# Gate and up: three of eight pairs of row tiles by seven products instead of two, with ScalarE copying the product banks out and GpSimd adding them

## The chip, the cores and the metric

The kernel runs on one core of a Trainium2 chip. The metric is the device time of one execution in microseconds (us). TensorE multiplies into PSUM (8 banks of 128x512 fp32), ScalarE (ACT) and VectorE (DVE) read PSUM and SBUF, GpSimd (POOL) works on SBUF, and SyncE (SP) issues the weight loads. Each engine has its own instruction stream, in order, and they meet at semaphores.

## The reference

The program is two layers of a four-mixer attention block and then one block with attention, convolution and a feed-forward part, on 256 tokens of width 2048. Only the feed-forward part matters here:

```python
h = rms_norm(x, norm2_g)                     # 256 x 2048
x = x + (silu(h @ w_gate) * (h @ w_up)) @ w_down   # w_gate, w_up: 2048 x 5632
```

All of it is fp32. A product of fp32 accuracy is made of three matmuls on rounded halves: high x high, high x low, low x high.

## The kernel before

**Tiling.** Gate and up are computed in 11 steps of 512 columns (`FFN_STEPS`). In a step the 2048 rows of a weight are 16 row tiles of 128, taken as 8 pairs. A load (`raw`, a ring of 4 buffers of 512 KB) brings one pair of one weight. ScalarE rounds it (`split_high`: `wh`), VectorE subtracts (`split_low`: `wl`), and TensorE multiplies. `wh` and `wl` are rings of 4 slots: the high part of unit n waits until unit n-4 is multiplied, the low part waits for the high part, the multiply waits for the low part. I call the two splits of unit n hi(n) and lo(n).

**An eight.** A pair of one weight is a unit of 12 matmuls of 512 columns. Both weights together need 24.

**A seven.** Steps 1 to 9 (`seven_step`) compute some pairs otherwise. The 2x2 blocks (two halves of the tokens by two row tiles) times (two row tiles by gate and up) are multiplied with seven products instead of eight (Winograd's form of Strassen): 21 matmuls for both weights. It takes four units, here called parts p0 to p3 (6, 3, 6 and 6 matmuls). p0 and p1 split raw weights. p2 and p3 split sums of weights that VectorE forms in `sum_weights` after lo(p1), from both raw buffers of the pair, which are free only then (`weights_summed`). Four products are accumulated in banks 4 to 7, called mixes; the rest goes straight to the accumulators of gate (banks 0, 1) and up (banks 2, 3).

**A step before.** 20 units: g0 g1 u0 u1, transposes, g2 u2, seven S0 (units 6 to 9), g3 u3, seven S1 (12 to 15), g4 g5 u4 u5. The eight transposes (`turn_act`) bring the product of the previous step into banks 4 and 5; ScalarE and VectorE read them out as `ah` (`act_turned`) and `al` (`act_low`). TensorE waits for both before it writes the mixes:

```python
if n == FIRST_SEVEN:                       # unit 6
    pe.wait_ge(act_mid_done, pl.slots + 2)
    pe.wait_ge(dve_mid_done, pl.slots + 2)
```

After S1 ScalarE copies one mix bank (`first_mix`), VectorE adds the others (`add_mixes`), adds the accumulators (`gate_sum`, `up_of_mixes`), ScalarE applies silu, and VectorE forms the product.

**Loads.** SyncE issues the loads of a step in the order of `plan.raws`. Load k waits for the one 4 places earlier to be done with: an eight's by its low part, a seven's two by its weight sums. The order is one queue, so a load that waits holds every later one.

## Time and profile before

| what | value |
|---|---|
| median of three runs | 1956.89 us (1956.38 to 1957.09) |
| the profiled execution | 1956.36 us, span of the core 1954.6 us |
| TensorE busy | 1939.9 us (99% of the span) |
| VectorE, ScalarE, GpSimd busy | 1365.2, 1000.6, 80.0 us |
| granted TensorE clock | 1.0 of full speed |
| the nine steps with sevens | from about 1284 us to 1673 us of the span |

Busy time of TensorE counts overlapping matmuls as one stretch. A row of the timeline is start, duration, engine, line, operation, out<-in, count, and in brackets the idle time ahead of it on that engine with the instruction that ended it.

### The profile page before, as it was taken

How to read it: one execution, taken by the hardware profiler on the slowest of the kernel's cores; microseconds unless marked ns; L12 is line 12 of the kernel's file. 1: busy time of each engine (PE TensorE's matmuls, PEld its weight loads, DVE VectorE, ACT ScalarE, POOL GpSimd, SP SyncE). 2: the span in 40 equal slices, each digit the busy share in tenths (PEclk: the TensorE clock that was granted, in tenths of full speed). 3: DMA queues.
4: the chain of work that ended last, by engine and by line, in shares of the span. 5: the costliest groups of instructions: out<-in, count | busy, mean ns of one | idle time of the engine just before them, and what ended most of it. 6: DMA issues, size and time to landing. Idle time of an engine off the chain costs nothing.

```text
span 1954.6 us, 26389 instructions
## 1 busy us (share of the span) xinstructions
PE 1939.9 (99%) x9568; PEld 1621.3 (83%) x9568; DVE 1365.2 (70%) x1619; ACT 1000.6 (51%) x1328; POOL 80.0 (4%) x125
## 2 busy tenths in 40 slices
PE   9999999999999999999999999999999999999998
PEld 7888888887888888888787878888888888888887
DVE  6595655556667664655657986768888888678777
ACT  6365444444555453444555555645555555445453
...
PEclk9999999999999999999999999999999999999999
...
GB/s 288 199 228 130 155 169 167 185 202 162 256 183 187 148 132 176 183 195 192 144 194 156 151 145 168 184 179 196 202 194 188 193 192 194 205 183 194 226 199 157
DMA packets 204538, 360.75 MB, mean 185 GB/s; under 512 B 13201, under 2 KB 53184, under 8 KB 204176
## 3 DMA queue, kind: packets, MB, share of 16 engines
...
q8 instruction: 65, 1.06, 0.2%
...
## 4 chain that ended last, share of the span: by engine, by line
PE 97%; ACT 1%; DVE 1%; DMA 0%; issue 0%; ACTq 0%; SPq 0%; DVEq 0%
PE psum L758 23%; PE psum L760 23%; PE psum L759 23%; PE psum L765 6%; PE psum L767 3%; PE psum L1305 2%; PE psum L1307 2%; PE psum L1306 2%; PE psum L1551 1%; PE psum L874 1%; PE psum L1239 1%; PE psum L888 1%; PE psum L863 1%; PE psum L1020 1%; PE psum L1808 0%; PE psum L782 0%
## 5 line engine op out<-in xcount | busy, mean ns | idle before, releaser
L723 DVE TENSOR_TENSOR wl<-raw,wh 128x1024 fp32r<-128x1024 f32 (+2 forms) x595 | 694.7, 1192 | 341.4 <-ACT wh L715 327.9
L715 ACT ACTIVATE wh<-raw 128x1024 fp32r<-128x1024 f32 (+2 forms) x595 | 603.1, 1032 | 536.0 <-PE psum L760 386.9
L758 PE MATMUL psum<-wh,xs 128*128 128x512 f32 (+2 forms) x1440 | 559.4, 389 | 4.5 <-DVE xs L1058 4.2
L760 PE MATMUL psum<-wh,xs 128*128 128x512 f32 (+2 forms) x1440 | 552.9, 384 | 0.0
L759 PE MATMUL psum<-wl,xs 128*128 128x512 f32 (+2 forms) x1440 | 552.5, 384 | 0.0
L758 PEld LDWEIGHTS psum<-wh,xs 128*128 128x128 f32 x1440 | 270.6, 188 | 60.8 <-DVE xs L1058 7.1
L760 PEld LDWEIGHTS psum<-wh,xs 128*128 128x128 f32 x1440 | 270.5, 188 | 53.0
L759 PEld LDWEIGHTS psum<-wl,xs 128*128 128x128 f32 x1440 | 270.8, 188 | 51.2
L765 PE MATMUL psum<-xs,wh 128*128 128x512 f32 x512 | 181.4, 398 | 0.0
L767 PE MATMUL psum<-xs,wl 128*128 128x256 f32 x512 | 143.3, 280 | 0.0
L758 PE MATMUL psum<-wh,mh 128*128 128x512 f32 x360 | 141.6, 393 | 0.0
L760 PE MATMUL psum<-wh,ml 128*128 128x512 f32 x360 | 140.2, 389 | 0.0
L759 PE MATMUL psum<-wl,mh 128*128 128x512 f32 x360 | 140.1, 389 | 0.0
L765 PEld LDWEIGHTS psum<-xs,wh 128*128 128x128 f32 x512 | 96.1, 188 | 22.4
L767 PEld LDWEIGHTS psum<-xs,wl 128*128 128x128 f32 x512 | 96.7, 189 | 0.1
L758 PE MATMUL psum<-wh,ah 128*128 128x512 f32 x248 | 96.6, 389 | 0.0
L760 PE MATMUL psum<-wh,al 128*128 128x512 f32 x248 | 96.5, 389 | 0.0
L759 PE MATMUL psum<-wl,ah 128*128 128x512 f32 x248 | 96.5, 389 | 0.0
L1332 DVE TENSOR_TENSOR wl<-raw,wh 128x1024 fp32r<-128x1024 f32 (+1 forms) x60 | 56.2, 956 | 37.4 <-ACT wh L1325 37.4
L1325 ACT ACTIVATE wh<-raw 128x1024 fp32r<-128x1024 f32 (+1 forms) x60 | 50.8, 847 | 59.0 <-PE psum L760 44.0
L758 PEld LDWEIGHTS psum<-wh,mh 128*128 128x128 f32 x360 | 67.6, 188 | 14.3 <-issue 0.6
L760 PEld LDWEIGHTS psum<-wh,ml 128*128 128x128 f32 x360 | 67.6, 188 | 14.3
...
## 6 DMA issues: line engine op xcount, KB each, us to landing
...
```

What stands on the lines that cost most here:

```text
L715: act.activation(shaped(wh[:, n % SPLIT_SLOTS], unit)[:, 0:k, 0:unit.n], shaped(buffer, unit)[:, 0:k, 0:unit.n], ACT.Copy).then_inc(hi_don ...
L723: dve.tensor_tensor(out=shaped(wl[:, n % SPLIT_SLOTS], unit)[:, 0:k, 0:unit.n], in0=shaped(buffer, unit)[:, 0:k, 0:unit.n], in1=shaped(wh[ ...
L758: pe.matmul(o, ah_[:, kt, tok], hi_w, start=first, stop=False)
L759: pe.matmul(o, ah_[:, kt, tok], lo_w, start=False, stop=False)
L760: ins = pe.matmul(o, al_[:, kt, tok], hi_w, start=False, stop=last)
L765: pe.matmul(o.rearrange("p (i t) -> p i t", i=2), hi_w[:, f], xs[:, :, kt, :], start=first, stop=False, skip_group_check=True)
L767: ins = pe.matmul(o[:, 0:T], lo_w[:, f], xh[:, kt, :], start=False, stop=last, skip_group_check=True)
L1305: pe.matmul(o, x_hi, hi_w, start=first, stop=False)
L1306: pe.matmul(o, x_hi, lo_w, start=False, stop=False)
L1307: ins = pe.matmul(o, x_lo, hi_w, start=False, stop=last)
L1325: act.activation(wh[:, n % SPLIT_SLOTS, 0:source.shape[1], :], source, ACT.Copy).then_inc(hi_done, 1)
L1332: dve.tensor_tensor(out=wl[:, n % SPLIT_SLOTS, 0:k, :], in0=source, in1=wh[:, n % SPLIT_SLOTS, 0:k, :].bitcast(F32), op=ALU.subtract).then ...
```

## The change

Three of the eight pairs become sevens (pairs 1, 3, 5), in nine steps. Units of a step are now 24: 0 g0, 1 u0, transposes, 2 g1, 3 to 6 S0, 7 u1, 8 g2, 9 to 12 S1, 13 u2, 14 g3, 15 to 18 S2, 19 u3, 20 and 21 the halves of g4, 22 and 23 the halves of u4. The names g1, u1 and so on count the eights alone. The u of a pair is loaded ahead of the seven and used after it (`+u1` in the order). The transposes go to banks 6 and 7, and TensorE waits for `ah` and `al` at p2 of S0 (unit 5), the first part that writes these banks. ScalarE copies all four mix banks to SBUF, GpSimd makes the four additions of 512 columns and the last product of 1024 columns, and ScalarE multiplies the silu by the token's scale.

```diff
-GATE_UP_SEVENS = (3, 6)
-GATE_UP_ORDER = ("g0", "g1", "u0", "u1", "g2", "u2", "S0", "g3", "u3", "S1", "g4", "g5", "u4", "u5")
+GATE_UP_SEVENS = (1, 3, 5)
+GATE_UP_ORDER = ("g0", "u0", "g1", "+u1", "S0", "u1", "g2", "+u2", "S1", "u2", "g3", "+u3", "S2", "u3", "G4", "U4")
...
-FIRST_SEVEN, SEVENS_END, GATE_END = 6, 16, 18
+FIRST_SEVEN, SEVENS_END, GATE_END, TURN_UNITS = 3, 19, 22, 2
...
+            def pool_mix(i):
...
+                pool.wait_ge(s("act_mixes"), 3 * (i - FIRST_SEVEN_STEP) + 1)
+                stand_alone(pool, "pool")
+                add(1, 0, 1)
+                pool.drain()
+                pool.wait_ge(s("act_mixes"), 3 * (i - FIRST_SEVEN_STEP) + 2)
+                stand_alone(pool, "pool")
+                add(2, 2, 1)
+                pool.drain().then_inc(s("pool_mixes"), 1)
+                add(1, 3, 1)
+                add(3, 3, 2)
+                pool.drain().then_inc(s("pool_mixes"), 1)
+                pool.wait_ge(s("act_mixes"), 3 * (i - FIRST_SEVEN_STEP) + 3)
+                pool.wait_ge(dve_mid_done, ffn_place(i + 1).slots + 1)
+                stand_alone(pool, "pool")
+                pool.tensor_tensor(out=act_a[:, :, :], in0=x_mixes[:, 1:4:2, :], in1=silu[:, :, :], op=ALU.mult)
+                pool.drain().then_inc(s("pool_mixes"), 1)
...
             def seven_step(i):
                 pl = ffn_place(i)
                 for n, unit in enumerate(GATE_UP.units):
-                    if n == 2:
+                    if n == 1:
                         pe.wait_ge(dve_mid_done, pl.slots + 1)
                     if n == FIRST_SEVEN:
+                        pe.wait_ge(s("sums_low"), 1)
+                    if n == FIRST_SEVEN + 2:
                         pe.wait_ge(act_mid_done, pl.slots + 2)
                         pe.wait_ge(dve_mid_done, pl.slots + 2)
-                        pe.wait_ge(s("sums_low"), 1)
...
-                    if n == SLOT_UNITS - 1:
+                    if n == TURN_UNITS - 1:
+                        if not isinstance(i, int):
+                            pe.wait_ge(s("pool_mixes"), 3 * (i - FIRST_SEVEN_STEP))
                         pe_stage(pl, 0, turn_act)
...
-            def first_mix(pl):
+            def copy_mixes(pl):
 
                 act.wait_ge(unit_used, SPLIT_SLOTS + pl.units + SEVENS_END)
-                act.activation(x_mixes[:, 0, :], psum[:, 4, :], ACT.Copy).then_inc(s("first_mix"), 1)
+                act.activation(x_mixes[:, 0:2, :], psum[:, 4:6, :], ACT.Copy).then_inc(s("act_mixes"), 1)
+                act.activation(x_mixes[:, 2:4, :], psum[:, 6:8, :], ACT.Copy).then_inc(s("act_mixes"), 1)
...
-                    ins = act.activation(silu[:, tb, :], x_mixes[:, 2 * tb, :], ACT.Silu, scale=x_rstd[:, tb:tb + 1])
-                ins.then_inc(s("gate_ready"), 1)
+                    ins = act.activation(silu[:, tb, :], silu[:, tb, :], ACT.Silu, scale=x_rstd[:, tb:tb + 1])
+                act.drain()
+                for tb in range(TB):
+                    ins = act.activation(silu[:, tb, :], silu[:, tb, :], ACT.Copy, scale=x_rstd[:, tb:tb + 1])
+                ins.then_inc(s("act_mixes"), 1)
...
             def seven_step(i):
                 pl = ffn_place(i)
+                dve_mid(pl, -1, 0, up_part if isinstance(i, int) else lambda: up_of_mixes(i - 1))
                 for n, unit in list(enumerate(GATE_UP.units))[AHEAD:]:
                     if unit.part is None:
                         split_low(pl, n, unit)
                     else:
                         seven_low(pl, n, unit)
-                    if n == 2:
-                        dve_mid(pl, -1, 0, up_part if isinstance(i, int) else lambda: up_of_mixes(i - FIRST_SEVEN_STEP))
-                    elif n == 7:
-                        dve_mid(pl, 0, SLOT_UNITS, lambda: act_low(i))
-                    elif n == GATE_END - 1:
-                        add_mixes(i, pl)
+                    if n == 6:
+                        dve_mid(pl, 0, TURN_UNITS, lambda: act_low(i))
```

On VectorE, in the loop over the steps, from the low part of S0's p1 on. Before (`wl` is a low part, `x_weight_sums` the weight sums, `al` the read-out of the transposes):

```order
L1332 TENSOR_TENSOR wl<-raw,wh 128x512 [waits hi_done]
L1344 TENSOR_TENSOR x_weight_sums<-raw 128x1024
L1347 TENSOR_TENSOR x_weight_sums<-raw,x_weight_sums 128x512
L1349 TENSOR_TENSOR x_weight_sums<-raw,x_weight_sums 128x512
L836 REGISTER_ALU [waits unit_used]
L2400 ISA [waits stage_done,ffn_high]
L2400 TENSOR_TENSOR al<-psum,ah 128x1024
L1329 REGISTER_ALU
L1332 TENSOR_TENSOR wl<-x_weight_sums,wh 128x1024 [waits hi_done]
L1329 REGISTER_ALU
L1332 TENSOR_TENSOR wl<-x_weight_sums,wh 128x1024 [waits hi_done]
```

In the changed kernel:

```order
L1372 TENSOR_TENSOR x_weight_sums<-raw,x_weight_sums 128x512
L1352 REGISTER_ALU
L1355 TENSOR_TENSOR wl<-x_weight_sums,wh 128x1024 [waits hi_done]
L1352 REGISTER_ALU
L1355 TENSOR_TENSOR wl<-x_weight_sums,wh 128x1024 [waits hi_done]
L857 REGISTER_ALU [waits unit_used]
L2465 ISA [waits stage_done,ffn_high]
L2465 TENSOR_TENSOR al<-psum,ah 128x1024
L741 REGISTER_ALU
L744 TENSOR_TENSOR wl<-raw,wh 128x1024 [waits hi_done]
L741 REGISTER_ALU
L744 TENSOR_TENSOR wl<-raw,wh 128x1024 [waits hi_done]
```

`al` stood between the weight sums and the low parts of p2 and p3; now it stands behind both, and u1's low part (the first `wl<-raw` behind it) follows.

On TensorE, in the loop, at the first seven. Before, from the last matmul ahead of S0 on (`x_sum_high` is a sum of x blocks):

```order
L760 MATMUL psum<-wh,xs 128x512
L1952 REGISTER_ALU
L1301 REGISTER_ALU [waits sums_low,dve_mid_done,act_mid_done]
L1305 MATMUL psum<-wh,xs 128x512 [waits lo_done]
L1306 MATMUL psum<-wl,xs 128x512
L1307 MATMUL psum<-wh,xs 128x512
L1305 MATMUL psum<-wh,xs 128x512
L1306 MATMUL psum<-wl,xs 128x512
L1307 MATMUL psum<-wh,xs 128x512
L1301 REGISTER_ALU
L1305 MATMUL psum<-wh,x_sum_high 128x512 [waits lo_done]
```

In the changed kernel, from the last matmuls of S0's p0 on:

```order
L1328 MATMUL psum<-wh,xs 128x512
L1329 MATMUL psum<-wl,xs 128x512
L1330 MATMUL psum<-wh,xs 128x512
L1324 REGISTER_ALU
L1328 MATMUL psum<-wh,x_sum_high 128x512 [waits lo_done]
L1329 MATMUL psum<-wl,x_sum_high 128x512
L1330 MATMUL psum<-wh,x_sum_low 128x512
L2011 REGISTER_ALU
L1324 REGISTER_ALU [waits dve_mid_done,act_mid_done]
L1328 MATMUL psum<-wh,x_sum_high 128x512 [waits lo_done]
L1329 MATMUL psum<-wl,x_sum_high 128x512
```

The wait for `dve_mid_done`, which `al` raises, stood ahead of p0 and is now ahead of p2 (the second `x_sum_high` row with a wait).

On SyncE, in the loop, the loads ahead of and at S1. Before, from the load of g3 (load 8) on:

```order
L1399 REGISTER_ALU
L1402 DMA raw<-in_w_up_dram 128x2x512 [waits lo_done]
L1401 ISA
L1402 ISA [waits weights_summed]
L1402 DMA raw<-in_w_gate_dram 128x2x512
L1402 DMA raw<-in_w_up_dram 128x2x512 [waits weights_summed]
L1399 REGISTER_ALU
L1402 ISA [waits lo_done]
L1402 DMA raw<-in_w_gate_dram 128x2x512
L1399 REGISTER_ALU
L1402 ISA [waits lo_done]
L1402 DMA raw<-in_w_gate_dram 128x2x512
```

In the changed kernel, from the load of g2 (load 6) on:

```order
L1428 REGISTER_ALU
L1431 ISA [waits lo_done]
L1431 DMA raw<-in_w_gate_dram 128x2x512
L1428 REGISTER_ALU
L1431 DMA raw<-in_w_up_dram 128x2x512 [waits lo_done]
L1430 REGISTER_ALU
L1431 ISA [waits weights_summed]
L1431 DMA raw<-in_w_gate_dram 128x2x512
L1431 DMA raw<-in_w_up_dram 128x2x512 [waits weights_summed]
L1428 REGISTER_ALU
L1431 ISA [waits lo_done]
L1431 DMA raw<-in_w_gate_dram 128x2x512
```

Ahead of S1's two loads, which wait for S0's weight sums, now stands load 7 (u2), whose `lo_done` is that of unit 7 (u1), multiplied after S0. Before, the loads ahead of them (g3, u3) waited for units 4 and 5, which come before S0. Load 11 (u3) stands in the same way ahead of S2's two loads and waits for unit 13.

## Rows read from the trace of the kernel before

**Rows 1.** The page: span, busy time, granted clock, the chain that ended last.

```profile
span 1954.6 us, 26389 instructions
PE 1939.9 (99%) x9568; PEld 1621.3 (83%) x9568; DVE 1365.2 (70%) x1619; ACT 1000.6 (51%) x1328; POOL 80.0 (4%) x125
...
PEclk9999999999999999999999999999999999999999
...
PE 97%; ACT 1%; DVE 1%; DMA 0%; issue 0%; ACTq 0%; SPq 0%; DVEq 0%
```

**Rows 2.** Windows, one middle step: us, busy by engine, clock, DMA share, GB/s.

```profile
1402.90:1446.10 43.20, 43.20 (x195) 35.66 (x194) 35.53 (x35) 22.75 (x25) 0.00 (x0) 1.00 0.61 194
```

**Rows 3.** Timeline of TensorE, the same step: first matmul behind S1, first transpose.

```profile
1402.66 0.39 PE L758 MATMUL psum<-wh,xs 128*128 128x512 f32 x1
...
1424.43 0.27 PE L1239 MATMUL psum<-ident,act 128*128 128x128 f32 x1
```

**Rows 4.** Timeline of ScalarE, the same step.

```profile
1402.87 0.60 ACT L2334 ACTIVATE x_mixes<-psum 128x512 f32<-128x512 f32 x1 [1.39 <-PE psum L1307]
...
1411.12 1.34 ACT L2340 ACTIVATE silu<-x_mixes,small 128x512 f32<-128x512 f32 x2 [1.45 <-DVEq L839]
...
1421.90 1.06 ACT L1325 ACTIVATE wh<-raw 128x1024 fp32r<-128x1024 f32 x1 [1.66 <-PE psum L760]
1424.63 0.63 ACT L1325 ACTIVATE wh<-raw 128x512 fp32r<-128x512 f32 x1 [1.66 <-PE psum L760]
1425.67 1.03 ACT L2301 ACTIVATE ah<-psum 128x1024 f32 x1 [0.41 <-PE psum L1239]
...
1446.09 0.60 ACT L2334 ACTIVATE x_mixes<-psum 128x512 f32<-128x512 f32 x1 [1.39 <-PE psum L1307]
```

**Rows 5.** Timeline of VectorE, the same step.

```profile
1413.44 1.23 DVE L723 TENSOR_TENSOR wl<-raw,wh 128x1024 fp32r<-128x1024 f32 x1 [0.97 <-ACT wh L715]
1414.59 1.22 DVE L2400 TENSOR_TENSOR x_mixes<-psum,x_mixes 128x1024 f32<-128x1024 f32 x1
...
1423.00 1.23 DVE L1332 TENSOR_TENSOR wl<-raw,wh 128x1024 fp32r<-128x1024 f32 x1 [1.49 <-ACT wh L1325]
1425.29 0.69 DVE L1332 TENSOR_TENSOR wl<-raw,wh 128x512 fp32r<-128x512 f32 x1 [1.07 <-ACT wh L1325]
...
1428.20 0.69 DVE L1349 TENSOR_TENSOR x_weight_sums<-raw,x_weight_sums 128x512 f32<-128x512 f32 x1
1429.35 1.23 DVE L2400 TENSOR_TENSOR al<-psum,ah 128x1024 f32 x1 [0.46 <-issue]
1430.76 2.52 DVE L1332 TENSOR_TENSOR wl<-x_weight_sums,wh 128x1024 fp32r<-128x1024 f32 x2 [0.18 <-issue]
...
1439.90 0.69 DVE L1349 TENSOR_TENSOR x_weight_sums<-raw,x_weight_sums 128x512 f32<-128x512 f32 x1
1440.79 1.23 DVE L1332 TENSOR_TENSOR wl<-x_weight_sums,wh 128x1024 fp32r<-128x1024 f32 x1 [0.20 <-issue]
```

**Rows 6.** Timeline of TensorE's weight loads, at the first matmul of S0.

```profile
1430.79 0.19 PEld L1305 LDWEIGHTS psum<-wh,xs 128*128 128x128 f32 x1 [0.29 <-issue]
```

**Rows 7.** SyncE's queue, the loads of S1's pair; then each one's time to landing.

```profile
1429.09 0.37 SPq L1402 DMA_DIRECT2D raw<-in_w_gate_dram  x1
1429.56 0.41 SPq L1402 DMA_DIRECT2D raw<-in_w_up_dram  x1
...
DMA to landing us min/median/max: 3.8/3.8/3.8
...
DMA to landing us min/median/max: 4.6/4.6/4.6
```

**Rows 8.** Timelines of GpSimd and VectorE, where the two overlap and where they don't.

```profile
494.66 1.22 DVE L723 TENSOR_TENSOR wl<-raw,wh 128x1024 fp32r<-128x1024 f32 x1 [2.23 <-ACT wh L715]
...
494.86 1.08 POOL L974 TENSOR_SCALAR small<-small 128x1 f32<-128x1 f32 x1
...
497.46 0.19 POOL L974 TENSOR_SCALAR small<-small 128x1 f32<-128x1 f32 x1 [0.78 <-ACTq L1014]
...
1057.35 0.21 POOL L974 TENSOR_SCALAR small<-small 128x16 f32<-128x16 f32 x1 [75.17 <-DVEq L2751]
```

More of the change, by code:

```diff
@@ L115, in __init__ @@
         self.by_rows = False
-        self.raw = self.part = None
+        self.raw = self.part = self.half = None
 def slots_of(units):
@@ L238, in eight, with eight_in_halves @@
         unit = Unit(self.weights[g], ((0, GN),), kts, "t", g, self.operand, self.ktiles, first, last)
-        unit.raw = self.load(g, kts, len(self.units))
+        if (g, kts) not in self.raws:
+            self.load(g, kts, None)
+        unit.raw = self.raws.index((g, kts))
+        self.released[unit.raw] = len(self.units)
         self.units.append(unit)
+    def eight_in_halves(self, g, kts, last):
+        raw = self.load(g, kts, len(self.units) + 1)
+        for half, kt in enumerate(kts):
+            unit = Unit(self.weights[g], ((0, GN),), (kt,), "t", g, self.operand, self.ktiles, False, last and half == 1)
+            unit.raw, unit.half = raw, half
+            self.units.append(unit)
     def seven(self, j):
@@ L287, in __init__ @@
                 self.seven(int(kind[1]))
+            elif kind[0] in "GU":
+                pair = eights[int(kind[1])]
+                self.eight_in_halves("GU".index(kind[0]), (2 * pair, 2 * pair + 1), pair == eights[-1])
+            elif kind[0] == "+":
+                pair = eights[int(kind[2])]
+                self.load("gu".index(kind[1]), (2 * pair, 2 * pair + 1), None)
             else:
@@ L713, in split_high @@
             act.wait_ge(unit_used, place.units + n + 1)
-            k = len(unit.kts)
+            k, k0 = len(unit.kts), unit.half or 0
             act.activation(shaped(wh[:, n % SPLIT_SLOTS], unit)[:, 0:k, 0:unit.n],
-                           shaped(buffer, unit)[:, 0:k, 0:unit.n], ACT.Copy).then_inc(hi_done, 1)
+                           shaped(buffer, unit)[:, k0:k0 + k, 0:unit.n], ACT.Copy).then_inc(hi_done, 1)
         def split_low(place, n, unit):
@@ L1292, in of_sum @@
             def of_sum(which):
+                if unit.operand == "x" and unit.pair == 2:
+                    return x_sum_high_2[:, which, :], x_sum_low_2[:, which, :]
                 return sum_h[:, unit.pair, which, :], sum_l[:, unit.pair, which, :]
@@ L1397, in load_plan @@
                     before = k - RAW_SLOTS if k < RAW_SLOTS else plan.released[k - RAW_SLOTS]
-                    if isinstance(before, int):
+                    if plan is GATE_UP and k < 2 and not isinstance(i, int):
+                        sp.wait_ge(s("weights_summed"), (i - FIRST_SEVEN_STEP) * (2 * len(GATE_UP_SEVENS)))
+                    elif plan is GATE_UP and k < RAW_SLOTS and not isinstance(i, int):
+                        sp.wait_ge(lo_done, RAW_SLOTS + place.units + plan.released[k - RAW_SLOTS] - len(plan.units) + 1)
+                    elif isinstance(before, int):
                         sp.wait_ge(lo_done, RAW_SLOTS + place.units + before + 1)
@@ L1930, in turn_act @@
             def turn_act():
-                return pe_turn_mix(act_a, 0)
+                return pe_turn_mix(act_a, 2)
             def ffn_step(i, first):
@@ L1944, in ffn_step @@
                         h = FFN_SLOT_ENDS.index(n + 1)
+                        if h == 0 and not first:
+                            pe.wait_ge(s("pool_mixes"), 3 * N_SEVEN_STEPS)
                         pe_stage(pl, h, turn_act if h == 0 and not first else nothing)
```

71 lines of the change are left out of this document (37 added, 34 removed).

## The prediction

> **What bounds the kernel now.** I read the page first: TensorE is busy for 1939.9 of 1954.6 us, the chain that ended last is TensorE for 97%, and the granted clock is full throughout [rows 1]. So time goes where matmuls go, or where the change makes TensorE wait. Then the window of one middle step: 43.2 us, TensorE busy for all of it, VectorE for 35.5, ScalarE for 22.8 [rows 2]. The copy of the first mix starts at 1402.87 and at 1446.09 [rows 4], so a step takes 43.22. From the first matmul behind S1 to the first transpose there are 96 matmuls in 1424.43 - 1402.66 = 21.77 us [rows 3]: 0.2268 each. The 186 matmuls of a step are 42.18 us, the transposes and one small wait 1.04. Last I read in the timelines how far ahead of TensorE the splits and loads run, for that is what the new order uses up.
>
> **What is saved.** The third seven takes 21 matmuls for 24: 3 x 0.2268 = 0.68 us a step, 6.1 us over nine steps. That is the whole gain: whatever moves off VectorE was covered by TensorE, which never waited for it there. About 0.2% of the time (3.9 us) is what a measurement of this kernel tells from no change.
>
> **Wait 1, p2 of S0 for `al`.** p2 now waits for `al`, and on VectorE `al` stands behind the low part of p3, unit 6. Its high part needs unit 2 multiplied, and between the end of unit 2 and p2 TensorE has only p0 and p1, 9 matmuls, 2.04 us. The chain: unit 2 of before ends 12 matmuls ahead of 1424.43, at 1421.71, and ScalarE starts at 1421.90, 0.19 later; VectorE starts at 1423.00, 1.10 later [rows 4, 5]; `al` can start 1.15 after a low part that is not followed by a drain (1413.44 to 1414.59), and takes 1.23 [rows 5]; the weight load behind it comes 0.21 after its end (1429.35 + 1.23 = 1430.58, then 1430.79, the small wait of before) [rows 5, 6], the matmul 0.1 later. Sum 3.98 us, so at least 1.94 us of stall. With the 0.46 that `al` stood idle for [rows 5] it is 2.3.
>
> A second chain ends there too. Let T be the end of the last seven. TensorE alone would reach p2 at T + 8.16 (u3 and four halves) + 5.44 + 1.03 + 2.72 + 2.04 = T + 19.4. VectorE's gate sum can start once g4 is done (T + 5.4), behind the low part of the next g0, whose load now comes late: about T + 7.1 to 8.3. Then ScalarE: two silus 1.34 [rows 4], a drain, two scaled copies at about 0.6 each, to T + 11.0; only then hi(2), so lo(2) at T + 12.15. VectorE then works without a gap: lo(2), lo(3) 1.15 each, lo(4) 0.69, weight sums 2.91 (from the end of p1's low part, 1425.29 + 0.69, to 1428.20 + 0.69), 0.2, lo(5) and lo(6) 1.15 each: `al` starts at T + 20.5, ends at T + 21.8, and p2 starts at T + 22.05 [rows 5]. Stall 2.65. I take **2.6 us a step**, bounds 1.9 and 3.0.
>
> **Wait 2, p2 of S1 for its loads.** SyncE's load 7 waits for lo(7), u1, which VectorE reaches only behind `al`; loads 8 and 9, S1's pair, stand behind it, though their buffers came free with S0's sums. Before, these loads went out 0.20 after the sums (1428.89, 1429.09) and landed 3.8 and 4.6 after their issue, at 1432.9 and 1434.2 [rows 5, 7]: each further 512 KB about 1.3 us later. Now three go out together, so I put the landing of load 9 at 0.2 + 3.8 + 2 x 1.3 = 6.4 to 6.6 us after lo(7). From there: high part to the start of p1's low part 0.66 (1424.63 to 1425.29), low part 0.69, sums 2.91, gap 0.20, low part of p2 1.23 [rows 4, 5], start of TensorE 0.15: 12.4 us after lo(7). lo(7) itself ends 0.18 + 1.23 after `al` [rows 5]. So from p2 of S0 to p2 of S1: 1.4 - 0.3 + 12.4 = 13.5 us. TensorE's work between them is 12 + 24 + 9 = 45 matmuls, 10.2. **Stall 3.3**. If load 7 delays the pair by one transfer less, 2.0; if the three land as slowly as 8 us, 4.8.
>
> **Wait 3, p2 of S2, the same way.** Load 11 waits for lo(13), u2, behind lo(11) and lo(12): 1.15 each after p2 of S1 can start, 2.3. Then the same 12.4, less 0.15: 14.5 against 10.2. **Stall 4.3**, bounds 3.0 and 5.8.
>
> **The loads elsewhere.** The last load of a step waits for lo(19) and holds the next step's first two. I counted that in the gate sum's start above. u4's halves need load 15 at about T + 3.5 and are multiplied from T + 5.4 on: covered by u3 and g4.
>
> **GpSimd.** No row shows an addition of 512 columns. Its two-operation instruction takes 0.19 us for one column and 0.21 for sixteen [rows 8]: 1.3 ns a column, so 0.87 us for 512 with one input. Two inputs read one after the other give 1.5, and 2.9 for the last product of 1024. I take these, the dearer, and 0.9 and 1.6 as the lower bound. The first two additions end at T + 4.6, ahead of the gate sum. The product starts at about T + 11.1, when the scaled silu and the up sum are there, and ends by T + 14.0 against the transposes at T + 13.6: hidden by wait 1, which is later. The Trainium skill (GPSIMD Engine Reference, section 3.1) gives 4497 ns for an fp32 add of 2048 columns; by that an addition of 512 is an estimated 1.1 us and the product 2.2, and the transposes would not wait at all. ScalarE's copies are 2 x 1.03 by the `ah` row [rows 4], beside u3.
>
> **Sum.** 2.6 + 3.3 + 4.3 = 10.2 us of stall, less 0.68 saved and about 0.1 of the old wait: +9.4 us a step, a step of 52.7. Nine steps: +85 us on the profiled execution's 1956.4 (its span is 1.8 less; the median of the runs is 0.5 more). **Predicted 2042 us**, slower by 4.3%. Its own range from the bounds of the three waits (6.9 to 13.6 a step less 0.8) is 2011 to 2072.
>
> **Rivals.**
> - *VectorE waits for GpSimd too.* GpSimd's small instruction took 1.08 us where it began during a low part that ended at 495.88, and ended with it (495.94); elsewhere 0.19 [rows 8]. So a low part holds GpSimd off. No row shows the reverse, since GpSimd's reads of 1 to 16 columns are too short. If each addition holds the low parts off in turn, the gate sum and lo(2) come later: the additions alternate with low parts from T + 2.8 on and put the gate sum at about T + 8.2, and the product (to T + 14) blocks lo(2) from T + 12.15: 1.5 to 3 us more on wait 1, +13 to +27 us, about 2062. The Trainium skill (SBUF — State Buffer, "SBUF: two separate sides") states such a lock for a VectorE instruction with two SBUF inputs against a GpSimd one that reads SBUF; the first half of it the trace bears out.
> - *Only wait 1 is real.* If loads run ahead more than I read (7 and 11 go out before VectorE holds them), waits 2 and 3 vanish: 9 x (2.6 - 0.8) = +16, 1972. Against it: load 7 needs the buffer that u1 is split from, so it can't.
> - *The clock falls.* TensorE would idle 2 to 4 us three times a step. The clock stayed full in this trace [rows 1], which has no such idle. At the lower of the two levels a matmul takes twice as long; where it falls on the stretch behind p2 of S2, which TensorE sets, 12 to 24 matmuls cost 2.7 to 5.4 us: +24 to +49, about 2078. The Trainium skill (TensorE: Matmul & The Clock Gate, Part 1) says that an idle TensorE drops to 1.2 GHz; nothing here shows it yet.
> - *Faster.* The splits keep ahead and only the 27 matmuls count: 1956.4 - 6.1 = 1950.3. One place decides: p2 of S0 would have to start within 2.04 us of unit 2's end, where the chain above is 3.98 by single rows. Only an order on VectorE other than the listed one could do it.
>
> **How the numbers follow.** Forecast 0.54, VectorE held off by GpSimd 0.24, clock 0.08, wait 1 alone 0.09, faster 0.04, no change 0.01. The range that leaves out no more than 2 in 10 holds the forecast and most of the lock: 2008 to 2088. Faster 0.04, same 0.01, slower 0.95, from the same cases.
>
> **What the changed kernel's profile would show.** A step of about 52.7 us between two copies of the mixes. TensorE idle ahead of the `x_sum_high` matmuls of p2, three times a step: at S0 for `al` (2.6), at S1 and S2 for lo(11) and lo(17) (3.3, 4.3). SyncE's three loads in a burst 0.2 us behind lo(7) and lo(13), the third landing over 6 us after the first's issue. ScalarE idle for a load at p0 and p1 of S1. Additions on GpSimd of 0.9 to 1.5 us, the product of 1.6 to 2.9. Low parts longer than 1.23 us would show the lock. It is wrong if loads 8 and 9 go out right behind S0's sums, or if the stalls at S1 and S2 are under 1 us.

## The result, and the profile after

The changed kernel takes **2082.59 us** (median of 4 runs, 2078.13 to 2083.84), the kernel before 1956.66 beside it (4 runs, 1956.38 to 1957.09): ratio 1.0638, 95% interval 1.0625 to 1.0651, 126 us slower. The profiled run took 2083.16 us. The forecast was 2042, range 2008 to 2088.

Lines of the page of the changed kernel: span, busy times, the two rows by slice for TensorE and its clock, the chain that ended last.

```profile
span 2081.1 us, 26673 instructions
PE 1974.8 (95%) x9541; PEld 1632.2 (78%) x9541; DVE 1399.5 (67%) x1638; ACT 1040.9 (50%) x1392; POOL 159.2 (8%) x170
PE   9999999999999999999999999878888788899999
...
PE 76%; DVE 8%; DMA 6%; issue 4%; DVEq 3%; ACT 2%; ACTq 1%; SPq 1%; POOL 0%; POOLq 0%
```

TensorE was 97% of the chain before [rows 1] and is 76% now; VectorE and the loads took the rest, and TensorE's row falls to 7 and 8 in the slices of the seven steps. One step, seen in ScalarE's timeline, from a copy of the mixes to the next, with the two waits for loads between (start, duration, engine, line, operation, and in brackets the idle time before it and what ended that):

```profile
1508.26 1.03 ACT L2395 ACTIVATE x_mixes<-psum 128x1024 f32<-128x1024 f32 x1 [0.96 <-PE psum L1330]
...
1538.10 1.06 ACT L1348 ACTIVATE wh<-raw 128x1024 fp32r<-128x1024 f32 x1 [6.07 <-DMA raw<-in_w_gate_dram]
1539.95 0.63 ACT L1348 ACTIVATE wh<-raw 128x512 fp32r<-128x512 f32 x1 [0.79 <-DMA raw<-in_w_up_dram]
...
1554.90 0.63 ACT L1348 ACTIVATE wh<-raw 128x512 fp32r<-128x512 f32 x1 [0.87 <-DMA raw<-in_w_up_dram]
...
1565.28 1.02 ACT L2395 ACTIVATE x_mixes<-psum 128x1024 f32<-128x1024 f32 x1 [1.81 <-PE psum L1330]
```

The step takes 57.02 us, against 43.22 [rows 4]. The nine steps are not alike: the eight distances between copies run from 54.68 to 60.66. With ScalarE 0.19 behind, T (the end of the last seven) is 1508.07 and 1565.09. The window of that step, and TensorE's waits from the end of the step before on:

```profile
1508.30:1565.30 57.00, 48.23 (x192) 37.97 (x191) 39.06 (x36) 27.17 (x32) 8.98 (x5) 0.91 0.44 148
```

```profile
1503.70 0.79 PE L1328 MATMUL psum<-wh,x_sum_high 128*128 128x512 f32 x1 [2.58 <-DVE wl L1355]
1517.31 0.49 PE L779 MATMUL psum<-wh,xs 128*128 128x512 f32 x1 [0.92 <-issue]
1531.69 0.79 PE L1328 MATMUL psum<-wh,x_sum_high 128*128 128x512 f32 x1 [2.98 <-DVEq L860]
1545.69 0.50 PE L1328 MATMUL psum<-wh,x_sum_high 128*128 128x512 f32 x1 [0.73 <-DVE wl L1355]
1555.34 0.50 PE L1328 MATMUL psum<-wh,xs 128*128 128x512 f32 x1 [1.20 <-DVE wl L1355]
1560.64 0.50 PE L1328 MATMUL psum<-wh,x_sum_high 128*128 128x512 f32 x1 [2.94 <-DVE wl L1355]
```

The `x_sum_high` rows behind a wait are p2 of S0 (1531.69), of S1 (1545.69) and of S2 (1560.64); 1517.31 is g0, which waited for the gate sum. VectorE in the same step, the low parts (L744), the gate sum, `al`:

```profile
1511.65 1.49 DVE L744 TENSOR_TENSOR wl<-raw,wh 128x512 fp32r<-128x512 f32 x1 [0.21 <-ACT wh L736]
1513.44 1.94 DVE L744 TENSOR_TENSOR wl<-raw,wh 128x1024 fp32r<-128x1024 f32 x1 [0.30 <-ACT wh L736]
1515.30 1.21 DVE L2465 TENSOR_TENSOR silu<-psum,x_mixes 128x1024 f32<-128x1024 f32 x1
...
1520.31 2.77 DVE L744 TENSOR_TENSOR wl<-raw,wh 128x1024 fp32r<-128x1024 f32 x1 [1.25 <-ACT wh L736]
...
1530.20 1.22 DVE L2465 TENSOR_TENSOR al<-psum,ah 128x1024 f32 x1
1531.62 2.36 DVE L744 TENSOR_TENSOR wl<-raw,wh 128x1024 fp32r<-128x1024 f32 x2 [0.20 <-issue]
```

GpSimd beside it, and SyncE's burst of loads behind lo(7) (a fourth load follows at 1534.62):

```profile
1509.46 1.29 POOL L1549 TENSOR_TENSOR x_mixes<-x_mixes 128x512 f32<-128x512 f32 x1 [44.04 <-ACT x_mixes L2395]
1511.05 1.54 POOL L1549 TENSOR_TENSOR x_mixes<-x_mixes 128x512 f32<-128x512 f32 x1 [0.30 <-issue]
1512.77 3.75 POOL L1549 TENSOR_TENSOR x_mixes<-x_mixes 128x512 f32<-128x512 f32 x2 [0.18 <-issue]
1519.60 2.40 POOL L1565 TENSOR_TENSOR act<-x_mixes,silu 128x1024 f32<-128x1024 f32 x1 [3.07 <-ACT silu L2405]
```

```profile
1532.87 0.37 SPq L1431 DMA_DIRECT2D raw<-in_w_up_dram  x1
1533.49 0.37 SPq L1431 DMA_DIRECT2D raw<-in_w_gate_dram  x1
1533.96 0.42 SPq L1431 DMA_DIRECT2D raw<-in_w_up_dram  x1
```

lo(2) began at 1520.31 while GpSimd's product ran and ended 1.08 behind it: 2.77 us for an operation that takes 1.23 alone [rows 5]. The windows around p2 of S0 and behind p2 of S2 (length, busy time of PE, PEld, DVE, ACT and POOL with their counts, granted clock, DMA share, GB/s):

```profile
1531.00:1537.00 6.00, 5.31 (x13) 4.16 (x14) 2.78 (x3) 1.03 (x2) 0.00 (x0) 0.50 0.47 158
1537.00:1538.00 1.00, 1.00 (x5) 0.82 (x4) 0.00 (x0) 0.00 (x0) 0.00 (x0) 0.66 0.97 352
1562.00:1564.00 2.00, 2.00 (x6) 1.52 (x6) 1.95 (x3) 0.63 (x1) 0.00 (x0) 0.50 0.05 7
```

TensorE was idle for 2.98 us, and the clock then stood at 0.50, the lower level of 1.2 GHz, until 1537; behind p2 of S2 it stood there from 1562 to 1564.

The clock does not fall in every step. Two steps on it stayed full behind p2 of S2 (1617.23), and there g0 waited for 2.40 us. TensorE's waits in that step, the window behind p2 of S2, and VectorE's three low parts and gate sum ahead of g0:

```profile
1617.23 0.50 PE L1328 MATMUL psum<-wh,x_sum_high 128*128 128x512 f32 x1 [2.57 <-DVE wl L1355]
1630.83 0.49 PE L779 MATMUL psum<-wh,xs 128*128 128x512 f32 x1 [2.40 <-issue]
1645.20 0.49 PE L1328 MATMUL psum<-wh,x_sum_high 128*128 128x512 f32 x1 [3.00 <-DVEq L860]
```

```profile
1617.20:1620.10 2.90, 2.87 (x12) 2.37 (x13) 2.90 (x4) 1.86 (x3) 0.00 (x0) 1.00 0.00 0
```

```profile
1623.89 5.00 DVE L744 TENSOR_TENSOR wl<-raw,wh 128x512 fp32r<-128x512 f32 x3 [3.24 <-ACT wh L736]
1628.82 1.21 DVE L2465 TENSOR_TENSOR silu<-psum,x_mixes 128x1024 f32<-128x1024 f32 x1
```

### The profile page after: what moved, and what is told of

It reads as the page before. It is cut to its first block, busy times and chain, and to the rows that moved or that the text cites. A ratio compares the mean times of both kernels' runs of the same rounds, so it can differ in the third digit from the quotient of the medians.

```text
span 2081.1 us, 26673 instructions
## 1 busy us (share of the span) xinstructions
PE 1974.8 (95%) x9541; PEld 1632.2 (78%) x9541; DVE 1399.5 (67%) x1638; ACT 1040.9 (50%) x1392; POOL 159.2 (8%) x170
## 4 chain that ended last, share of the span: by engine, by line
PE 76%; DVE 8%; DMA 6%; issue 4%; DVEq 3%; ACT 2%; ACTq 1%; SPq 1%; POOL 0%; POOLq 0%
PE psum L779 18%; PE psum L781 17%; PE psum L780 17%; PE psum L786 6%; DMA raw<-in_w_up_dram 4%; PE psum L788 3%; DVE wl L744 2%; DVE wl L1355 2%; DMA raw<-in_w_gate_dram 2%; DVEq L860 2%; DVE x_weight_sums L1367 2%; PE psum L1328 1%; PE psum L1329 1%; PE psum L1330 1%; DVEq L1366 1%
## 5 line engine op out<-in xcount | busy, mean ns | idle before, releaser
L744 DVE TENSOR_TENSOR wl<-raw,wh 128x1024 fp32r<-128x1024 f32 (+2 forms) x595 | 704.3, 1207 | 364.4 <-ACT wh L736 351.7
L736 ACT ACTIVATE wh<-raw 128x1024 fp32r<-128x1024 f32 (+2 forms) x595 | 586.9, 1005 | 504.0 <-PE psum L781 342.8
L779 PE MATMUL psum<-wh,xs 128*128 128x512 f32 (+2 forms) x1368 | 534.2, 390 | 19.5 <-issue 15.3
L780 PE MATMUL psum<-wl,xs 128*128 128x512 f32 (+2 forms) x1368 | 525.9, 384 | 0.0
L781 PE MATMUL psum<-wh,xs 128*128 128x512 f32 (+2 forms) x1368 | 525.5, 384 | 0.0
L779 PEld LDWEIGHTS psum<-wh,xs 128*128 128x128 f32 x1368 | 258.2, 189 | 77.7 <-issue 20.2
L781 PEld LDWEIGHTS psum<-wh,xs 128*128 128x128 f32 x1368 | 257.8, 188 | 50.7
L780 PEld LDWEIGHTS psum<-wl,xs 128*128 128x128 f32 x1368 | 258.2, 189 | 48.4
L1355 DVE TENSOR_TENSOR wl<-raw,wh 128x1024 fp32r<-128x1024 f32 x78 | 74.6, 980 | 112.2 <-ACT wh L1348 112.0
L1348 ACT ACTIVATE wh<-raw 128x1024 fp32r<-128x1024 f32 x78 | 66.0, 847 | 154.1 <-DMA raw<-in_w_gate_dram 108.0
L1328 PE MATMUL psum<-wh,x_sum_high 128*128 128x512 f32 x108 | 52.8, 489 | 65.6 <-DVE wl L1355 40.8
L1348 ACT ACTIVATE wh<-x_weight_sums 128x1024 fp32r<-128x1024 f32 x54 | 57.2, 1059 | 89.2 <-DVEq L1369 71.0
```

The source lines that it names most:

```text
L736: act.activation(shaped(wh[:, n % SPLIT_SLOTS], unit)[:, 0:k, 0:unit.n], shaped(buffer, unit)[:, k0:k0 + k, 0:unit.n], ACT.Copy).then_inc( ...
L744: dve.tensor_tensor(out=shaped(wl[:, n % SPLIT_SLOTS], unit)[:, 0:k, 0:unit.n], in0=shaped(buffer, unit)[:, k0:k0 + k, 0:unit.n], in1=shap ...
L779: pe.matmul(o, ah_[:, kt, tok], hi_w, start=first, stop=False)
L780: pe.matmul(o, ah_[:, kt, tok], lo_w, start=False, stop=False)
L781: ins = pe.matmul(o, al_[:, kt, tok], hi_w, start=False, stop=last)
L1328: pe.matmul(o, x_hi, hi_w, start=first, stop=False)
```

## The experiments

"Step" is the mean distance of two copies of the mixes, from the second copy to the eighth, in each kernel's own profile; the first distance is left out, since the first step has a wait of its own wherever GpSimd has work in it (last section). For the changed kernel it is (1733.62 - 1391.43) / 6 = 57.0, for the kernel before 43.2. The best a step with three sevens can do is 183 matmuls, 41.5, and transposes, 1.04: 42.5.

| kernel | us | ratio (95%) | step |
|---|---|---|---|
| the change | 2082.6 | 1.0638 (1.0625 to 1.0651) | 57.0 |
| e1 `al` early | 2081.7 | 1.0642 (1.0625 to 1.0658) | 56.8 |
| e8 additions on VectorE | 2077.5 | 1.0617 (1.0599 to 1.0635) | 55.8 |
| e4 GpSimd on one column | 2064.6 | 1.0552 (1.0536 to 1.0568) | 54.6 |
| e2 new order | 2010.4 | 1.0272 (1.0256 to 1.0287) | 49.0 |
| e3 new order, `al` behind p2 | 2001.3 | 1.0226 (1.0212 to 1.0240) | 48.0 |
| e5 = e3, gate sum first | 1987.0 | 1.0151 (1.0134 to 1.0168) | 46.0 |
| e6 = e3, additions on VectorE | 1985.6 | 1.0149 (1.0132 to 1.0166) | 45.7 |
| e7 = e5 and e6 | 1982.5 | 1.0130 (1.0113 to 1.0147) | 45.7 |
| e9 = e7, weight sums first | 1999.0 | 1.0215 (1.0201 to 1.0229) | 47.7 |
| e10 = e9, nothing on GpSimd | 1982.6 | 1.0133 (1.0118 to 1.0149) | 46.1 |
| e12 = e7, nothing on GpSimd | 1970.8 | 1.0067 (1.0054 to 1.0081) | 44.8 |
| e11 = e12, S2 behind u3, up additions later | 1965.2 | 1.0040 (1.0026 to 1.0054) | 44.2 |

### e1, e2, e3: order of work

e1 (on ScalarE; VectorE's `n == 6` for `al` likewise), and the edit of e2, which has `n == 7`, still behind p3 of S0; e3 is e2 with `n == 6`:

```diff
-                    elif n == 6:
+                    elif n == 4:
```
```diff
-GATE_UP_ORDER = ("g0", "u0", "g1", "+u1", "S0", "u1", "g2", "+u2", "S1", "u2", "g3", "+u3", "S2", "u3", "G4", "U4")
+GATE_UP_ORDER = ("g0", "u0", "g1", "u1", "S0", "g2", "u2", "S1", "g3", "+u3", "S2", "u3", "G4", "U4")
```

> The changed kernel with one edit: ScalarE and VectorE form `ah` and `al` behind p1 of S0 (and its weight sums) and not behind p3. The full computation is kept. My theory of the changed kernel's time is that the order on VectorE makes wait 1 (p2 of S0 for `al`, 2.98 us in the step read) and the late loads make the rest. By it `al` is formed two low parts (2 x 1.15 us) earlier, so p2 of S0 starts about 2.3 us earlier, but now the low parts of p2 and p3 stand behind `al`, and p2's own low part ends where `al` ended less one low part: p2 gains 1.2 us, not 2.3. The loads follow lo(7), which does not move earlier since VectorE has the same work in front of it, so the waits at S1 and S2 grow by what S0 gave back. Theory 1 (late loads bound, in series): step within 0.5 us of the changed kernel's 57.6, time 2076 to 2083. Rival (each wait is its own): 1.2 us less a step, 2072. Rival (it is the clock alone that makes the loss big, and a shorter stall at S0 keeps it up): 3 us less a step or more, under 2056.

> The changed kernel with the order of the units alone changed: g0 u0 g1 u1 S0 g2 u2 S1 g3 S2 u3 g4 u4 (the load of u3 still ahead of S2's). The loads of S1 and S2 then wait for low parts that VectorE does before the sevens, not for u1's and u2's behind them. `al` is still formed behind p3 of S0. The same matmuls, the full computation. Theory (late loads make waits 2 and 3, and their stalls bring the clock down): the stalls at S1 and S2 go, and the clock's fall behind p2 of S2 with them. What stays: TensorE alone reaches p2 of S0 at T + 22.1 (one eight later than in the changed kernel), `al` behind p3 as before at T + 23.3 as measured, plus nothing else in front: p2 at T + 23.6, a stall of 1.5 us, plus perhaps 1.2 if the low part of u1 comes on top of it: 2.7. Step 44.0 to 45.2, time 1970 to 1981. Rival (loads are not the cause; GpSimd's hold on VectorE and the clock are): step over 50 us, time over 2015.

> The order of the units as in the last (g0 u0 g1 u1 S0 g2 u2 S1 g3 S2 u3 g4 u4), and `al` formed behind p2 of S0 and not behind p3, the full computation kept. Theory: one low part (1.15 us) less in front of `al` than with it behind p3, so the stall at p2 of S0 is 0.3 to 1.5 us, the others are gone, the clock stays full: step 42.5 + 0.3 to 1.5, time 1950 to 1963, so between a little faster than the kernel before and 0.3% slower. Rival (GpSimd holds VectorE's low parts by 2 us or more a step in any order): stall 2.5 us or more, 1970 and over. Rival (loads no cause): over 2015.

e1: same as the change, as the theory of waits in series has it: forming `al` sooner buys nothing where loads behind VectorE are next. In its profile p2 of S0 starts 22.8 behind T in most steps and not 23.6, and p2 of S1 comes 14.8 behind p2 of S0 and not 13.9. e2 took off 72 us. Its edit moves the loads and also puts one more eight ahead of S0, but its profile tells the two apart: from p2 of S0 to p2 of S1 it takes 10.3 us for TensorE's 10.2, and from there to p2 of S2 8.6 for 7.5, so waits 2 and 3 fall by 7.2 us a step, some 65 of the 72. The loads were the largest part. Yet both e2 and e3 missed what I expected, by 30 and 38 us. e3's waits in TensorE's timeline show why:

```profile
1466.72 0.50 PE L1328 MATMUL psum<-wh,x_sum_high 128*128 128x512 f32 x1 [1.37 <-DVE wl L1355]
1480.32 0.79 PE L779 MATMUL psum<-wh,xs 128*128 128x512 f32 x1 [2.37 <-issue]
```

In the step read p2 of S0 and S1 wait no more. What I had left out is g0 of the next step (1480.32). VectorE and GpSimd ahead of it:

```profile
1473.53 4.85 DVE L744 TENSOR_TENSOR wl<-raw,wh 128x512 fp32r<-128x512 f32 x3 [3.39 <-ACT wh L736]
1478.31 1.21 DVE L2465 TENSOR_TENSOR silu<-psum,x_mixes 128x1024 f32<-128x1024 f32 x1
```
```profile
1474.06 3.24 POOL L1549 TENSOR_TENSOR x_mixes<-x_mixes 128x512 f32<-128x512 f32 x2 [0.18 <-issue]
```

VectorE stood idle 3.39 us for the load of u4, and then three low parts took 4.85 us (0.69 + 0.69 + 1.23 alone, 2.6) beside GpSimd's additions; the gate sum came last. The clock went down behind the 2.37 us of idle, as in five of the seven steps after the first; in the other two it stayed full behind 2.40:

```profile
1479.00:1482.00 3.00, 1.69 (x4) 1.41 (x5) 2.81 (x3) 2.35 (x4) 0.00 (x0) 0.67 0.67 203
1482.00:1485.00 3.00, 3.00 (x11) 2.38 (x11) 1.76 (x2) 2.54 (x4) 2.41 (x1) 0.77 0.57 174
```

### e4 and e8: what GpSimd costs in the order of the change

```diff
-  pool.tensor_tensor(out=x_mixes[:, out_, :], in0=x_mixes[:, a, :], in1=x_mixes[:, b, :],
+  pool.tensor_tensor(out=x_mixes[:, out_, 0:1], in0=x_mixes[:, a, 0:1], in1=x_mixes[:, b, 0:1],
```

and the product likewise. It leaves out nearly all of the adding and of the product. e8 takes the four additions out of `pool_mix` and puts them on VectorE, behind the low part of unit 21.

> The changed kernel with GpSimd's four additions and its product made on one column of 512 and not on all. This leaves out nearly all of the adding of the four banks and of the product with silu; what follows reads what stood in those buffers. Everything else, the order on every engine too, is kept. It shows what GpSimd's time and its hold on VectorE's two-input instructions cost. Theory (hold shown in the trace: lo(2) of one step took 2.77 us and not 1.22, the gate sum's start moved to T + 7.2 and the up sum's to T + 9.8): 1.5 to 2.5 us a step of wait 1 go, and the 0.92 before u0; late loads follow VectorE, so they move with it but their waits stay: step 57.6 - 2.5 to 3.5, time 2051 to 2060. Rival (VectorE's delay at S0 is hidden behind the late loads' waits, in series): under 0.5 us a step, 2078 and over. Rival (the hold alone makes the loss): under 2000.

> The changed kernel in its own order of units, with one part undone: the four additions back on VectorE, behind ScalarE's copies; GpSimd keeps the product. Full computation. It shows what moving the additions to GpSimd gave or cost. With GpSimd's work cut to one column the time fell by 18 us; that took away the hold of the additions and that of the product. Theory (the hold costs as much as the additions): the low parts behind the last seven are not held, 1 to 2 us a step earlier, of which the late loads behind take part: 2060 to 2075. Rival (moving them paid, as the new order leaves VectorE no time): 2.8 us a step more, 2095 to 2108. Rival (both cancel): 2078 to 2084.

With GpSimd's work gone the step is 2.4 us shorter, 18 us in all; e4 came in 5 us above the range expected. The additions on VectorE gave 5 us, with intervals that overlap, and that sum hides two things. The step is 1.3 us shorter, and the first step is 4.0 longer (64.68 us from copy to copy for 60.66). The stretch from p2 of S2 to the next p2 of S0 shows what GpSimd costs, by the clock behind p2 of S2:

| p2 of S2 to the next p2 of S0 | clock full | clock fallen |
|---|---|---|
| the change | 28.0 | 28.0 to 28.1 |
| e8 | 26.2 to 26.3 | 27.4 to 27.6 |
| e4 | 25.1 to 25.6 | 26.1 to 26.2 |

(Steps from the second on; left out is the one in each kernel in which the clock was down for all of p2 and p3 of S2.) Making the additions on GpSimd and not on VectorE cost 1.7 us a step where the clock was full and 0.5 where it fell, having the product there and not at all 0.8 and 1.3. Which of the two makes most of the 18 us these runs don't tell.

### e5, e6, e7: the wait at g0

```diff
-                step_ahead(i + 1, 0)
                 dve_mid(pl, 1, GATE_END, lambda: gate_sum(i))
+                step_ahead(i + 1, 0)
```

is e5; e6 has the additions on VectorE as in e8; e7 both.

> The new order of units with `al` behind p2 (the kernel of 2001.3 us), and on VectorE the gate sum ahead of the low part of the next step's g0. Full computation. In that kernel the step read takes 48.0 us; the next step's g0 waits 2.37 us for the gate sum (it ends at T + 10.5, T the end of the last seven), TensorE's clock reads 0.67 and 0.77 in the two stretches behind, about 1.7 us of matmul time, and p2 of S2 waits 1.14. Theory (the late load of u4 and GpSimd's hold on the low parts of u4 make VectorE late, 3.39 us idle and then three low parts in 4.85 us): the gate sum goes from third to second place, but the low part of g0, which the same matmul wants, comes behind it: both done at T + 10.6: 0 to 0.5 us a step less, 1997 to 2001. Rival (the place of the gate sum alone is at fault): 2.4 us and the clock's 1.7 a step less, 1964.

> The kernel of 2001.3 us with the four additions of the mixes back on VectorE, behind ScalarE's two copies, at the place where VectorE stands idle for 3.4 us waiting for the load of u4; GpSimd keeps the product. Full computation. Theory (GpSimd's hold costs VectorE as much as the additions themselves: three low parts in 4.85 us and not 2.6, two in 3.91 and not 2.4): VectorE's additions take about 2.8 us from T + 1.9 on, the low parts end at T + 7.5, the gate sum at T + 8.7, so g0 of the next step waits 0.6 us and the clock holds: 3.5 us a step less, 1965 to 1973. Rival (VectorE is full, so 2.8 us more work on it show up at S1 and S2): 1995 to 2025.

> The same with both edits: additions on VectorE, and the gate sum ahead of the low part of the next g0. Full computation. Theory: gate sum at T + 6.4 to 7.6, the low part of g0 to T + 8.8, TensorE needs it at T + 8.9: no wait there, the clock full. Left is up to 1.1 us at p2 of S2, which shrinks if VectorE comes to the sevens earlier: step 42.6 to 43.8, time 1951 to 1962. Rival (VectorE full): 1990 and over.

e5 gave 14.4 us where I expected about 4 at most and the rival 37: the wait at g0 fell from 2.37 to 0.83 in the step read and the clock stayed up, which I had not counted. e6 gave 15.7 (expected 28 to 36), e7 only 3.1 more. None of the ranges held. In e3 the stretch from p2 of S2 to the next p2 of S0 takes 27.97 us in the two steps whose clock stayed full behind g0 and 28.9 to 29.2 in the five where it fell; in e6, with the clock full, 26.1 to 26.5. So of what e6 gave a step some 1.7 is the hold and the place of the additions, and 1.1, in five steps of seven, the clock. In e7 the waits of TensorE are

```profile
1473.50 0.50 PE L779 MATMUL psum<-wh,xs 128*128 128x512 f32 x1 [0.28 <-DVE wl L744]
1488.05 0.49 PE L1328 MATMUL psum<-wh,x_sum_high 128*128 128x512 f32 x1 [0.40 <-DVEq L860]
1507.46 0.50 PE L1328 MATMUL psum<-wh,x_sum_high 128*128 128x512 f32 x1 [1.40 <-DVE wl L1355]
```

The last, p2 of S2, is a round trip. Its stations in ScalarE's timeline (high parts of p1 of S1 and of p0 of S2) and in SyncE's:

```profile
1491.11 0.64 ACT L1348 ACTIVATE wh<-raw 128x512 fp32r<-128x512 f32 x1 [0.32 <-PE psum L1330]
...
1500.15 1.06 ACT L1348 ACTIVATE wh<-raw 128x1024 fp32r<-128x1024 f32 x1 [1.17 <-DMA raw<-in_w_gate_dram]
```
```profile
1496.27 0.37 SPq L1431 DMA_DIRECT2D raw<-in_w_gate_dram  x1
1496.74 0.42 SPq L1431 DMA_DIRECT2D raw<-in_w_up_dram  x1
```

p3 of S0 leaves its place in the ring at 1490.9, p1 of S1 takes it (1491.11), VectorE's low part and sums free the buffers, S2's loads go out at 1496.27, and p2 of S2 starts at 1507.46: 16.5 us, where TensorE has 66 matmuls, 15.0.

### e9, e10, e12: the round trip, and the product

```diff
+                        if unit.part == 0:
+                            ...
+                            sum_weights(GATE_UP.units[n + 1])
-                        seven_low(pl, n, unit)
+                        seven_low(pl, n, unit, False)
```

is e9's (with SyncE waiting for p1's low part too). e10 and e12 form the product as before:

```diff
+                tt(x_mixes[:, 1:4:2, :], acc[1], x_mixes[:, 1:4:2, :], ALU.add).then_inc(s("pool_mixes"), 1)
+                ...
+                    dve.scalar_tensor_tensor(out=act_a[:, tb, :], in0=x_mixes[:, 1 + 2 * tb, :], scalar=x_rstd[:, tb:tb + 1],
+                                             in1=silu[:, tb, :], op0=ALU.mult, op1=ALU.mult)
```

> The kernel of 1982.5 us (new order of units, additions on VectorE, gate sum first) with one more edit: in each seven of gate and up VectorE forms the weight sums as soon as the pair of loads is there, ahead of the low parts of p0 and p1, and SyncE's loads into these buffers wait for p1's low part too. Full computation. In that kernel a step takes 45.6 us; TensorE waits 1.4 to 1.5 at p2 of S2, 0.4 at p2 of S0, 0.3 at the next g0. Theory (the wait at S2 is one round trip: p1's high part needs the place in the ring that p3 of the seven before leaves, then low part, sums, load of 4.6 us, low part, sums, p2; 16.4 us against TensorE's 66 matmuls, 15.0): the sums stand no longer behind p1's high and low parts, the buffers are free 1.4 us sooner, the wait at S2 falls to 0 to 0.3; 1 to 1.4 us a step, 1969 to 1974. Rival (VectorE is full, 40.1 of 45.4 us, so its order changes nothing): 1980 to 1984. Rival (the sums wait for the loads with p0's low part behind them, so p0 comes late instead): 1984 and over.

> The last kernel with nothing left on GpSimd: ScalarE copies one bank, VectorE adds the others from PSUM and forms the product with silu, as in the kernel before; three sevens, the new order, the gate sum first and the sums first stay. Full computation. Theory (in the step read the product of 2.40 us on GpSimd held two low parts to 4.19 us for 2.4: 1.8 us of VectorE's time lost, against 1.41 for making it there; ScalarE has 1.34 less): VectorE is 0.4 to 1 us earlier, the wait for `al` at S0 goes, the additions begin 0.6 us earlier and g0's wait of 0.3 goes: step 42.6 to 43.2, 1951 to 1957, at best 0.3% faster than before. Rival (GpSimd does pay here, VectorE full): 2 us a step more than the last kernel, 1990.

> The kernel of 1982.5 us (order g0 u0 g1 u1 S0 g2 u2 S1 g3 S2 u3 g4 u4, additions on VectorE, gate sum first, product on GpSimd) with one edit: the product and the last of ScalarE's work for it go back to where the kernel before had them, so nothing of gate and up is left on GpSimd; ScalarE copies one bank. The weight sums stand behind p1's low part. Full computation. With the kernel of 1999.0 and that of 1982.6 us, which have the sums first, this gives the product's price a second time. Theory (GpSimd's product holds VectorE for 1.8 us a step and costs it more than making it, 1.41; the wait at p2 of S2 is the round trip through ring and loads and stays): 1.4 to 1.6 us of wait left at p2 of S2, none at S0; step 44.2 to 44.6, 1966 to 1971. Rival (VectorE is full in the whole middle of the step, so what it is spared comes off the wait at S2 too): the wait at S2 under 1.2 us, 1958 to 1964. Rival (the product is as dear on either engine): 1980 to 1984.

e9 was 16.6 us slower than e7, the third rival's case: the sums wait for the pair and p0's low part behind them, and p0 of S2 is late instead, in e9's timeline by

```profile
1466.80 0.50 PE L1329 MATMUL psum<-wh,xs 128*128 128x512 f32 x1 [2.26 <-DVE wl L1356]
```

In e10 the same wait is 2.04, and behind it the clock falls (to 0.67 from 1501 to 1504), which it does not in the steps read of e7 and e12:

```profile
1498.00:1501.00 3.00, 2.46 (x8) 1.98 (x9) 3.00 (x4) 0.56 (x2) 0.00 (x0) 0.76 0.00 0
```

So e10 missed as well; e12, which leaves the sums where they were, came in at 1970.8 (expected 1966 to 1971) with a step of 44.8 (44.2 to 44.6), and the wait of the round trip is there, about as long as expected (1.4 to 1.6):

```profile
1496.23 0.50 PE L1328 MATMUL psum<-wh,x_sum_high 128*128 128x512 f32 x1 [1.37 <-DVE wl L1355]
```

Taking the product off GpSimd gave 11.6 us without the sums first and 16.4 with them, though VectorE then has 1.41 us more to do a step. Neither is the hold's price alone. In the profiled executions, which lie 13.0 and 21.0 us apart, the first step makes 7.9 and 10.5 of it (52.35 to 44.50, and 56.13 to 45.67), for in e7 and e9 the transposes wait there once for GpSimd (last section). The other steps give 0.9 and 1.6 us each. And the edit takes more than the product: ScalarE copies one bank for four and no longer scales the silu, and VectorE adds from PSUM. What each is worth was not separated.

### e11: S2 behind u3

```diff
+GATE_UP_ORDER = ("g0", "g1", "u0", "u1", "S0", "g2", "u2", "S1", "g3", "u3", "S2", "G4", "U4")
```

The order also takes g1 ahead of u0. Beside it VectorE makes the additions for the up part only ahead of the up sum, so e11 differs from e12 in more than the place of S2.

> Three sevens in another order, drawn from what the last kernels showed: g0 g1 u0 u1 S0 g2 u2 S1 g3 u3 S2 g4 u4. Nothing on GpSimd; ScalarE copies one bank, VectorE adds the others, but the additions for the up part come only ahead of the up sum, and the gate sum ahead of the low part of the next g0; weight sums behind p1's low part as in the changed kernel. Full computation. Between p3 of S0 and p2 of S2 there are now 78 matmuls, 17.7 us, where the round trip (ring, low part, sums, load, low part, sums, p2) takes 16.4: no wait at p2 of S2. Behind S2 only four halves are left, 5.44 us. Theory (the round trip sets the wait at S2; VectorE is full only if nothing behind S2 lets it catch up): the gate sum ends at T + 4.3, the low part of the next g0 at T + 5.7, so g0 waits 0.4 us: step 42.9 to 43.4, 1953 to 1959. Rival (VectorE is the bound wherever S2 stands; it is now asked for 36 us of work within a shorter stretch): 1 to 2 us at p2 of S0 or of S1, 1966 to 1976. Rival (the cover behind S2 is too short, as copy, additions and gate sum take T + 7 in the kernel before): 1.5 to 3 us at g0, 1970 to 1985, with the clock falling.

The fastest with three sevens, 5.6 us below e12, 8 above the kernel before, and 6 above the range expected (1953 to 1959). The round trip's wait is gone: p2 of S1 to p2 of S2 takes 10.2, TensorE's own 45 matmuls. Left are

```profile
1460.28 0.50 PE L779 MATMUL psum<-wh,xs 128*128 128x512 f32 x1 [0.29 <-DVE wl L744]
1475.30 0.49 PE L1328 MATMUL psum<-wh,x_sum_high 128*128 128x512 f32 x1 [0.76 <-DVEq L860]
```

so `al` at S0 is a little late, with VectorE at work without a gap from the gate sum on: half of the first rival. From T to p2 of S0 it takes 20.9 us, and TensorE alone would need 19.4: the two cost 1.5 us, over twice the 0.68 that the third seven saves. No version beat the kernel before.

## Why the prediction was right, and its size was not

The direction and the mechanism held: three waits for VectorE, two of them for loads stuck behind a late low part. By its steps, beside the step read and the mean of the six steps from the second T on (1391.24 to 1733.43):

| stretch | forecast | step read | mean |
|---|---|---|---|
| T to p2 of S0 | 22.05 | 1531.69 - 1508.07 = 23.62 | 24.1 |
| p2 of S0 to p2 of S1 | 13.5 | 14.00 | 13.9 |
| p2 of S1 to p2 of S2 | 14.5 | 14.95 | 15.0 |
| p2 of S2 to T | 2.72 | 1565.09 - 1560.64 = 4.45 | 4.05 |
| step | 52.8 | 57.0 | 57.0 |

- **Saved, 0.68 a step**: held in the count, 183 matmuls for 186.
- **Clock.** It fell behind p2 of S2 in five of eight steps, and yet cost next to nothing. Where it stayed full (p2 of S2 to T 2.87 to 2.89), the next stretch, T to p2 of S0, took 25.1; where it fell (4.35 to 4.45), 23.6. Both together are 27.96 to 28.08 in six steps of seven, 28.95 in the one in which p2 of S2 to T took 5.34. With a full clock TensorE comes to g0 sooner and waits 2.40 there for the gate sum; with a fallen clock 0.50 to 0.95. So VectorE sets this stretch, and not TensorE, as the rival had it at 2.7 to 5.4 us. In the mean it cost 0.2. Behind p2 of S0 it is the same: 13.58 us to p2 of S1 in a step with a full clock and 2.77 us of idle time, and 13.58 in one with a fallen clock and 0.32. The Trainium skill (TensorE: Matmul & The Clock Gate, Part 1) has an idle TensorE drop to 1.2 GHz; the windows at 0.50 agree, though not behind every idle time (last section).
- **Wait 1.** This is the term that was sized too small. From p2 of S2 over T to the next p2 of S0 the forecast is 2.72 + 22.05 = 24.8, measured 28.0: 3.2 missing. The second chain ended it, and it was late in two places. The gate sum started 11.6 behind p2 of S2 in the step read and in that at 1617.23 alike, for 9.8 (T + 7.1): the three low parts ahead of it took 5.00 for 2.6 beside GpSimd's additions (1623.89). That put lo(2) 16.6 behind, for 14.9. Then lo(2) took 2.77 for 1.23, beside the product: 1.54 more. It was the rival "VectorE waits for GpSimd too", with 1.5 to 3 us; e4, with GpSimd's work gone, is 2.4 to 2.8 shorter in this stretch where the clock is full, so that much of the 3.2 is the hold. The rest is the load of the next g0: in e4 its high part still waits for it, and there the gate sum starts at T + 7.4 (1614.53 in e4's timeline; forecast 7.1 to 8.3). The Trainium skill (SBUF — State Buffer, "SBUF: two separate sides") states this lock; the trace agrees, 2.77 for 1.23. g0's wait, which I had put at nothing, lies inside this stretch.
- **Waits 2 and 3.** The loads went out in bursts at 1532.87 and later. Load 9 was used at 1539.95, 7.1 us behind lo(7), for 6.4 to 6.6: about 0.5 us each time. e2 showed these waits' weight. One sign of being wrong did show: I had written that a stall at S1 or S2 of under 1 us would refute this, and p2 of S1 waited only 0.73 in the step read and 0.32 in another. The length of the stretch held all the same. TensorE ran part of its 45 matmuls there at half clock and so filled the wait; idle time was the wrong thing to name, the length from one p2 to the next the right one.
- **GpSimd.** Additions of 1.29 (0.9 to 1.5) and the product of 2.40 (1.6 to 2.9): held. That the product hides held for TensorE's transposes, not for VectorE.
- **Sum.** In the mean 3.2 for the stretch of wait 1, most of it GpSimd's hold, 0.2 for the clock, 0.4 and 0.5 for the loads make 4.3 us a step, 38 over nine, and 3.6 in the first step (60.66 for 57.03) make 42 of the 41 missing. What was mis-sized is wait 1: the hold stood beside the sum as a case of its own, at a chance of 0.24, and belonged in it.
- **The range.** The one worked out from the three waits, 2011 to 2072, did not hold. That of 2008 to 2088 did, because it had been drawn wide enough to take in most of the rival's case.
